# Hybrid attention block: order of the first maxima and of the sliding tables, and the last batch's scaling moved into the merge

## The reference

```python
h = rms_norm(x) * (1 + scale) + shift              # scale, shift, gate from c
q, k, v, f, z | qb, kb, vb, zb | ga, gb = h @ w_in
# branch A (FoX): 8 heads of 64, causal, decay from the forget gate
logits = q.k / 8 + F[t] - F[s];   ya = (softmax(logits) @ v * silu(za)) @ w_o_fox
# branch B (sliding): 8 query heads, 2 key heads, chunks of 64, window of 2 chunks,
# ALiBi penalty and a learned sink per head
yb = (softmax([qb.kb / 8 - slope * dist, sink]) @ vb * silu(zb)) @ w_o_swa
out = x + gate * ((sigmoid(ga) * ya + sigmoid(gb) * yb) @ w_out)
```

## Time and profile before

| | us |
|---|---|
| median of 3 runs | 2127.08 (2125.26 to 2133.05) |
| profiled execution | 2127.95 |
| its span | 2126.2 |
| PE busy in the span | 1979.7 (93%) |
| DVE, ACT, POOL busy | 885.6, 737.5, 550.5 |

### The profile page before, as it was taken

The page is one execution under the profiler, slowest core; times in us unless marked ns, Lnnn a source line. Parts: engine busy times, 40 slices in busy tenths (PEclk is TensorE's granted clock), DMA queues, the critical chain, the costliest instruction groups (busy, mean ns, idle before and its releaser), DMA issues. The chain is left out here.

```text
span 2126.2 us, 27983 instructions
## 1 busy us (share of the span) xinstructions
PE 1979.7 (93%) x9722; PEld 1555.5 (73%) x9722; DVE 885.6 (42%) x1851; ACT 737.5 (35%) x1375; POOL 550.5 (26%) x502
## 2 busy tenths in 40 slices
PE   7389999999999999999989899999999959998998
PEld 2368778798788788888866566666666639997887
DVE  2945555562212220000234455555565335554332
ACT  2622222220112132121115677767777751002000
POOL 1600000000000000000004576767777742110000
PEclk9589999999999999999986999999999979999999
DMA  6233443345512212121424446446464334232322
GB/s 238 98 101 89 120 119 99 118 133 136 134 50 89 78 49 89 49 89 58 124 74 95 96 112 159 113 92 144 108 141 99 74 122 137 80 99 99 119 91 77
DMA packets 235435, 222.63 MB, mean 105 GB/s; under 512 B 54610, under 2 KB 188498, under 8 KB 234292
## 3 DMA queue, kind: packets, MB, share of 16 engines
q1 hardware_dynamic: 221892, 180.95, 30.8%
q0 software_dynamic: 11648, 39.85, 5.9%
q10 hardware_dynamic: 1792, 0.53, 0.1%
HBM read 149.18 MB, written 71.70 MB: 104 GB/s over the span
## 5 line engine op out<-in xcount | busy, mean ns | idle before, releaser
L1242 POOL TENSOR_TENSOR Pl<-PT,Ph 128x512 fp32r<-128x512 f32 (+2 forms) x350 | 415.5, 1204 | 200.2 <-ACT Ph L1342 192.9
L474 PE MATMUL pj<-hTh,Wh 128*128 128x512 f32 x768 | 299.6, 390 | 0.7 <-DVE Wl L679 0.4
L475 PE MATMUL pj<-hTl,Wh 128*128 128x512 f32 x768 | 299.0, 389 | 0.0
L476 PE MATMUL pj<-hTh,Wl 128*128 128x512 f32 x768 | 298.9, 389 | 0.0
L474 PE MATMUL pj<-Wh,hTh 128*128 128x512 f32 (+1 forms) x640 | 246.1, 385 | 23.9 <-DVE Wl L679 23.9
L376 POOL DMA_DIRECT2D wraw<-in_w_in x84 | 45.1, 537 | 856.4 <-DVE Wl L679 850.3
L1335 ACT ACTIVATE PT<-sc 128x512 f32<-128x512 f32 (+2 forms) x350 | 192.6, 550 | 137.7 <-PE sc L1267 46.2
L476 PE MATMUL pj<-Wh,hTl 128*128 128x512 f32 (+1 forms) x640 | 240.0, 375 | 0.0
L475 PE MATMUL pj<-Wl,hTh 128*128 128x512 f32 (+1 forms) x640 | 239.9, 375 | 0.0
L1342 ACT ACTIVATE Ph<-PT 128x512 fp32r<-128x512 f32 (+2 forms) x350 | 207.9, 594 | 11.2
L1082 DVE TENSOR_REDUCE part_max<-mx 128x1 f32<-128x512 f32 (+3 forms) x267 | 157.6, 599 | 98.4 <-PE mx L1028 97.1
(11 more groups left out here) (231 smaller groups left out, 3553.5 us busy)
## 6 DMA issues: line engine op xcount, KB each, us to landing
qk_scratch<-qThl SPq DMA_DIRECT2D x96, 256.0 KB, 2.8
wraw<-in_w_in POOLq DMA_DIRECT2D x88, 256.0 KB, 3.8
g_scratch<-st SPq DMA_DIRECT2D x64, 256.0 KB, 2.4
gt<-g_scratch SPq DMA_DIRECT2D x16, 1024.0 KB, 7.8
xin<-in_x POOLq DMA_DIRECT2D x16, 512.0 KB, 5.0
wada<-in_w_ada SPq DMA_DIRECT2D x8, 1024.0 KB, 7.7
z_scratch<-st SPq DMA_DIRECT2D x32, 256.0 KB, 2.4
Qb<-qk_scratch SPq DMA_DIRECT2D x32, 256.0 KB
```

Source lines behind the costliest of these rows:

```text
L474: nc.tensor.matmul(out, a_hi, b_hi, start=first, stop=False)
L475: nc.tensor.matmul(out, a_hi, b_lo, start=False, stop=False)
L476: return nc.tensor.matmul(out, a_lo, b_hi, start=False, stop=last)
L1242: pool.tensor_tensor(Pl[n % NPH][0:rows, 0:w], PT[n % NP][0:rows, 0:w], Ph[n % NPH][0:rows, 0:w].bitcast(F32), ALU.subtract).then_inc(low_ ...
```

## The change

Four things:

- **Order at the stage's start.** The fourth FoX block's maxima no longer come in turns -3 to 6 but in turns 1 to 8, behind the first four scores. The sliding tables come at turns 4 to 9 instead of 1 to 6. The first head's sliding units are all in its fourth block (four units there, none in the third). SP's first loads are spread differently, with the sinks' load sixth instead of second.
- **A shorter lead for sliding maxima.** `TILE_LEAD` stays 16 for FoX and becomes 11 for sliding tiles. By the planner's numbers the row transpose of a sliding tile from the second on is now 5 turns ahead of the turn that scores it (10 before).
- **The last batch's scaling crosses the border.** `turns[-1]` is set beyond the loop and `TAIL` becomes 2. The merge issues the same instructions itself (`Finish`).
- **Four row tiles of w_o are loaded in the attention stage**, once block 27 is scored, into the places of the key tiles of even heads.

Buffers are placed by hand so that what crosses the border keeps its place (`R`, `rs`, `yl1`, `gt1`, the early rows).

```diff
-        units = ((0, 1, 1, 2) if i >= JB else (0, 0, 1, 3))[j]
+        units = ((0, 1, 1, 2) if i >= JB else (0, 0, 0, 4))[j]
...
-    TILE_LEAD, ROW_LAG, SPACING = 16, 3, {"f": 1.05, "s": 1.5}
-    TABLES_AT, TABLE_TURNS = 1, 6
+    TILE_LEAD, ROW_LAG, SPACING = {"f": 16, "s": 11}, 3, {"f": 1.05, "s": 1.5}
+    TABLES_AT, TABLE_TURNS = 4, 6
...
-    at = [None] * NU + [max(math.floor(due), START + u // 2) for u, (it, due) in enumerate(later)]
+    at = [None] * NU + [max(math.floor(due), 1 + u // 2) for u, (it, due) in enumerate(later)]
...
-    s_due = when((t, START + 1 + 7 * t if t < 2 else last["s", 2 * t - 3] + 1) for t in range(TT))
+    s_due = when((t, START + 4 + 11 * t if t < 2 else last["s", 2 * t - 3] + 1) for t in range(TT))
...
+    turns[-1] = NS + 1000
+    LAST = len(turns) - 1
-    TAIL = 28
+    TAIL = 2
...
+    def load_weights(sp):
+        sp.wait_ge(scored, last["f", (FOX_H - 1) * JB - 1] + 1)
+        for k, tile in enumerate(keep["early_rows"]):
+            sp.dma_start(tile, io["w_o_fox"][0, k * P:(k + 1) * P, :]).then_inc(keep["w_o_in"][k], 16)
```

In `merge`:

```diff
         @block.sync
+            finish.sums(sp)
             load(sp)
+            finish.inverses(sp)
...
         @block.gpsimd
+            low_y(0, 0, slice(BK, KT))
+            finish.wait(pool)
+            low_y(0, 1, slice(0, KT))
...
         @block.tensor
-            pe.wait_ge(y_split, 1)
             for k in range(KT):
                 pe.wait_ge(w_split, k + 1)
+                if k == BK:
+                    pe.wait_ge(y_split, 1)
...
         @block.scalar
-            high_y(0, 0)
-            for k in range(KT):
+            high_y(0, 0, slice(0, BK))
+            high(act, 0)
+            high_y(0, 0, slice(BK, KT))
+            for k in range(1, KT):
                 high(act, k)
...
         @block.vector
+            dve.wait_ge(y_hi, 1)
+            nc.vector.tensor_tensor(yl[0][:, 0:BK, :], yT[:, 0:BK, 0:TB], yh[0][:, 0:BK, :].bitcast(F32), ALU.subtract)
             for k in range(KT):
                 low(dve, k)
+                if k == 3:
+                    finish.invert(dve)
...
+            gate(0, 0, range(BK))
+            finish.scale(dve)
+            gate(0, 0, range(BK, KT))
+            gate(0, 1)
```

More of the change, by code:

```diff
@@ L939, in attention @@
     sb.free[-1][0] = TABLE_AT + 3936
+    sb.free[1][0] += 4 * QW * NZ
+    sb.free[-1][1] -= 128
+    rooms = [nc.alloc_sbuf_tensor_at(f"w_o_early{k}", [P, 2, D], F32, offset=at) for k, at in enumerate((RAW_AT, HOT_AT))]
+    keep["early_rows"] = [room[:, m, :] for room in rooms for m in range(2)]
     Ka, Kb = ([sb(f"{n}{k}", [P, S], F32R, next(at)) for k in range(2)] for n, at in (("Ka", ka_at), ("Kb", kb_at)))
@@ L1211, in _ @@
                     for k in sum_load(n):
[L1212 to L1216, removed]
+                        load_sums(sp, k)
                     for k in inv_load(n):
[L1218 to L1221, removed]
+                        load_inverses(sp, k)
                     for k in inv_store(n):
-                        sp.wait_ge(inverted, k + 1)
-                        sp.dma_start(dram["inv"][k].rearrange("m s (a n) -> (m s a) n", n=32), rs[:]).then_inc(inv_out, 16)
+                        store_inverses(sp, k)
             @block.gpsimd
@@ L1421, in collect @@
                     last_op.then_inc(y_done, 1)
[L1423 to L1436, removed]
                 set_up()
@@ L1488, in merge @@
         Wh, Wl = sb("woh", [P, KT, D], F32R), sb("wol", [P, KT, D], F32R)
-        yh, yl = ([sb(f"{n}{k}", [P, KT, TB], F32R) for k in range(2)] for n in ("yh", "yl"))
-        gates = [sb(f"gt{k}", [P, 2, KT, TB]) for k in range(2)]
+        gates = [sb("gt0", [P, 2, KT, TB]), sb("gt1", [P, 2, KT, TB], F32, HOT_AT)]
+        yh = [sb(f"yh{k}", [P, KT, TB], F32R) for k in range(2)]
+        yl = [sb("yl0", [P, KT, TB], F32R, HOT_AT + 16384), sb("yl1", [P, KT, TB], F32R, HOT_AT - 8192)]
+        sb.free[1][1] -= 8192
+        sb.free[2][0] += 8192
         ta, tb_ = [sb(f"ta{k}", [P, TB]) for k in range(2)], [sb(f"tb{k}", [P, TB]) for k in range(2)]
@@ L1497, in merge @@
         spare = gates[1].rearrange("p a k n -> p (a k n)")
-        ring = [t[:] for t in keep["w_raw"]] + [spare[:, c:c + D] for c in range(0, 2 * KT * TB, D)]
-        load, high, low, w_split = split_rows(nc, ctx, "m", sources, ring, Wh, Wl)
+        ring = keep["early_rows"] + [spare[:, c:c + D] for c in range(2 * D, 2 * KT * TB, D)]
+        load, high, low, w_split = split_rows(nc, ctx, "m", sources, ring, Wh, Wl, keep["w_o_in"])
         gate_in = [sem(f"m_g{k}") for k in range(2)]
@@ new lines, in gate @@
+            def gate(i, u, ms=range(KT)):
+                dve.wait_ge(gate_in[u], i * 32 + 32)
+                for m in ms:
+                    n = u * KT + m
+                    dve.wait_ge(mm_done, i * 2 * KT + (n + 1))
+                    dve.wait_ge(merged, i * PER + (PER + n - 1))
+                    nc.vector.tensor_tensor(ta[n % 2][:], pa[n % 4][:, 0:TB], gates[u][:, 0, m, :], ALU.mult)
+                    nc.vector.tensor_tensor(tb_[n % 2][:], pb[n % 4][:, 0:TB], gates[u][:, 1, m, :], ALU.mult).then_inc(gated, 1)
+                    dve.wait_ge(gated, i * PER + (n + 1))
+                    nc.vector.tensor_tensor(yT[:, m, bass.ds(i * 2 * TB + u * TB, TB)], ta[n % 2][:], tb_[n % 2][:],
+                                            ALU.add).then_inc(merged, 1)
@@ L1718, in build @@
     with ExitStack() as ctx:
-        keep = {"after_yT": YT_AT + 65536, "ident": ctx.enter_context(nc.sbuf_tensor("ident", [P, P], F32)),
+        keep = {"after_yT": YT_AT + 65536, "w_o_in": [ctx.enter_context(nc.semaphore(f"w_o_in{k}")) for k in range(4)], "ident": ctx.enter_context(nc.sbuf_tensor("ident", [P, P], F32)),
                 "siluc": ctx.enter_context(nc.sbuf_tensor("siluc", [P, KT], F32))}
@@ L1726, in build @@
             condition_and_norm(nc, io, keep)
-            early_part, attend = attention(nc, io, keep, dram, ctx)
+            early_part, attend, finish = attention(nc, io, keep, dram, ctx)
             project(nc, io, keep, dram, early_part)
@@ L1730, in build @@
         attend()
-        keep["w_raw"] = [ctx.enter_context(nc.sbuf_tensor(f"w_raw{k}", [P, D], F32)) for k in range(2)]
+        keep["w_raw"] = [nc.alloc_sbuf_tensor_at(f"w_raw{k}", [P, D], F32, offset=RAW_AT + k * 4 * D) for k in range(2)]
         keep["w_out_in"] = [ctx.enter_context(nc.semaphore(f"w_out_in{k}")) for k in range(2)]
-        merge(nc, io, keep, dram)
+        merge(nc, io, keep, dram, finish)
         output(nc, io, keep, dram, out)
```

103 lines of the change are left out of this document (70 added, 33 removed).

## The result

| | us |
|---|---|
| before, median of 4 runs | 2130.07 (2125.26 to 2139.47) |
| with the change, median of 4 runs | 2188.14 (2184.51 to 2190.67) |
| ratio | 1.027 (95% interval 1.0225 to 1.0307) |
| profiled execution, before and after | 2127.95 and 2190.67 |
| its span, before and after | 2126.2 and 2189.0 |

What follows compares the result with a forecast made beforehand. PE, the busiest engine, was taken as bound by its gaps and half-clock stretches at attention's start and the merge. Gains of 22 and 11, less 2 and 0.5, gave 30.5 us: from 2127.95 to 2097 us, range 2084 to 2111.

Steps and rivals of the forecast that it cites:

- Term C: Sliding tiles in attention: the shorter lead leaves rows 4.0 us to land; a loss of 2 us (0 to 12).
- the near rows: Small transfers at the merge, a store landing within 1.2 us and a load in 1.8, by which no sliding tile waits.
- The far end: Slowest landing considered for a sliding tile's rows: 7.4 us, from the start of R's load to its use.
- The rival: Sliding tiles: lead of five turns too short, 14 tiles each wait 2.4 us plus slow clock, 73 us lost, 2168; chance 0.03.
- Term A: Attention stage's start: fewer waits and less half clock, a gain of 22 us (about -2 to +31).
- the prediction's own sign of being wrong in A: At the attention stage's start: the clock row shows 0.50 for more than 15 us.
- The fill: Attention start: PE's wait after its first scores for ACT, POOL and DVE, taken as 1 us (0 to 3).
- The third tile's wait: Attention start: PE waits for the third sliding tile's load, 3.4 us (2 to 6.2).
- the 25 us stretch: Attention start, 1133 to 1158: half clock after the last sliding table's wait, costing 12.5 us, said to go.
- the ledger: Attention start, 1105.3 to 1211.4: sum of idle and half-clock losses, 37.7 us before and 15.5 us after.
- Term B: The merge: PE starts earlier but then stands about 9 us for the gates; a gain of 11 us (8 to 20).
- a border that gives nothing: Rival at the attention start or the merge: one of the two brings no gain, 2115 us; chance 0.06.

Runs made afterwards that it cites:

- e2: The kernel before with only the sliding lead cut from 16 to 11: 2200.4 us, ratio 1.031.
- e5: The kernel before with sliding maxima where they were and only the rows of tiles 2 to 15 moved 5 turns later: 2173.5 us, ratio 1.023.
- e4: The kernel before with the start part alone, lead 11 for sliding tiles 0 to 2 only and 16 for the others: 2130.6 us, ratio 1.001.
- e12: The changed kernel with sliding tiles 0 to 2 at lead 13, the others at 16, and K loads 3 turns apart: 2104.0 us, ratio 0.990.
- e8: The kernel before with the merge part (early w_o rows and new buffer places included) and a head's K loads 3 instead of 5 turns apart: 2108.2 us, ratio 0.991.
- e10: The kernel before with only a head's K loads 3 instead of 5 turns apart: 2115.4 us, ratio 0.995.
- e3: The changed kernel with the start's order and sliding lead 16 as before, leaving the merge part, early w_o rows and buffer places: 2122.0 us, ratio 0.996.
- e6: The changed kernel with the bytes of K loads (from head 2) and V loads (from head 1) cut to one partition, all still issued: 2148.2 us.

## Why the prediction was wrong

**Term C is the step that failed.** The prediction left 4.0 us for the rows to land after the last issue and took "the near rows": 1.2 and 1.8 us, landings at the merge with nothing else under way. It priced Term C at 2 us; the lead costs 70 (e2). The slack was read about rightly (tiles 5 and 9 are scored 3.3 and 3.4 us after the issue ended, with no wait). The landing was not. It is 6.2 to 7.7 us in the burst and 5.4 to 5.9 beside `R`. The far end that the prediction named, 7.4 us, has the right size by luck: it is two transfers of 512 KB at the merge with nothing else under way, and says nothing about how long 4 KB take among other loads. The sentence "with SP's loads on the same engines some will: 14 tiles at 0 to 0.9 us" priced the sharing without looking at what SP issues in those turns. In the kernel before, the rows of the even tiles were issued ahead of the next head's K, Q and V and used 12 us later, so its trace never showed a late one. Placing the rows' turn among SP's turns, tile by tile, would have shown that every second tile falls into the burst: the rows of tile 4 have turn 84, SP's loads for the next head turns 83, 86 and 88. This is no accident, since both follow the heads' period of 44 turns.

The sum that decides the case then reads: the rows' move 46 us (e5) and the maxima's move 24 us (what e2 costs beyond that: waits for keys and rows, and slow clock), together 70 instead of 2. The second part was nowhere in the prediction: moving the sliding maxima took away work that stood in front of a wait for K loads. The rival had the mechanism. Its price of 73 us is near the 70 partly by luck: how its 2.4 us per tile follow from 7.4 and 4.0 is not shown, and not 14 tiles wait alike but eleven, 0.5 to 5.3 us each. Its waits come to 14 x 2.4 = 33.6 us, and in after those eleven add up to 36.5. Its chance of 0.03 was low, given that the slack of 4.0 us lay between the near rows and the far one.

**Term A was wrong as well: 22 us forecast, 0 to 4 measured** (e4: none; e12 to e8: 4, neither clear of noise). Two executions with the same half clock from 1104 to 1240, e12 (12.5 us) and e10 (12.3), say the same: e12 is 3.5 us ahead at POOL's 51st low half (1217.8 against 1221.3). Piece by piece:
- The first score came 0.7 us after the time that was said (1106.7), and the wait for a table went.
- The clock is 0.50 from 1106 to 1125.5 in after, 19 us instead of 10.5, which is the prediction's own sign of being wrong in A (more than 15 us).
- The fill was put at 1 us with the sinks' load as its cause. PE's fourth maximum waited 2.3 us in after and 2.9 in e4 for DVE, which is busy with the set-up (pads, distances, memsets) from 1106.6 to 1117.7 almost without a gap (after waits 0.5 us for the sinks).
- The third tile's wait was 3.0 (3.4 forecast).
- The 12.5 us for the 25 us stretch were counted as if it belonged to the kernel. It belongs to that one execution: e10's has 11 us at the same place behind the same wait. Over the whole start, the six kernels with the old start (before, e2, e3, e5, e8, e10) lose 12 to 25 us to half clock from 1104 to 1240, and the eight with the new one 12 to 27.
- Tile 2's rows, moved only 5 turns ahead of the score, cost 4 to 5 us of wait and some 2.4 of slow clock (e4); that is Term C again, right behind Term A's stretch.
- "The work is the same matmuls in another order" held for the whole, but the ledger ended at block 4's first score, and maxima had been moved across that line (2.8 us of them, by e12).

**Term B was right in its mechanism and nearly in its size.** PE starts 5.0 us after attention's last work (4 to 5 forecast), stands 8.96 us before the fifth channel tile (9 forecast), and the gates' load starts 14.1 us after attention's last store (12.5 forecast). From the end of PE's last attention work to its going on behind the gates there are 28.2 us in after and 39.7 before: 11.5, against 11. From the start of POOL's last low half in attention to the end of the span, the six kernels without this part take 403.4 to 405.3 us and the eight with it 392.8 to 396.8, a gain of 9.4 on the mean. By the medians e3 gives 8 and e10 to e8 gives 7. No run took its pieces apart.

**The early w_o rows** cost nothing that shows: e8 and e12, which have them, have a clock of 1.00 from 1240 to 1700 and no wait above 1 us there. No run left out just these.

Two small sums of the prediction are off: all good ends of Term A give 32 us, not 31, and a border that gives nothing makes 2119 (the start) or 2108 (the merge), where 2115 stands. Neither bears on the result.

## What to carry to other kernels

Before a transfer's lead is cut, read its landing where it will be issued, in the turn and beside the loads that stand there, and not at a place where the queue is idle; a small transfer from a quiet engine waits for the loads of other engines that it falls among (here 6.2 to 7.7 us instead of 2.2 to 2.8). List what stands in front of each wait that moved work used to cover. And take a slow-clock stretch of one profile as a gain only when a second execution shows it with the same length.

## What the runs showed of the hardware

- Four transfers of 4 KB started by ACT had landed by 2.2 to 2.8 us after the last start with K's and V's bytes cut (e6, even tiles), and landed 6.2 to 7.7 us after it while SP loaded tiles of 128 and 256 KB (209 GB/s in all, around tile 6).
- A wait of 1.2 to 1.7 us for keys was enough, in some places, to be followed by 4 to 11 us at 0.50 (e3 at 1308, 1383 and 1458); behind the fourth of e3's waits, 1.20 us at 1610, nothing followed. The same wait at the same place (3.2 us at 1132) was followed by 11 us at half clock in one execution and by 25 in another.
- The scatter between the runs of one kernel goes with the clock: in the 52 runs of the kernel before (2118 to 2144 us) the mean granted clock lies between 0.955 and 0.969, and a straight line of 1.7 us per 0.001 accounts for 85% of the variance. What decides the length of a slow stretch stays open.
